# Six row buffers instead of eight for gathered expert rows in a hybrid decoder layer

## The chip, the cores and the metric

The kernel runs on one core of one Trainium2 chip. The metric is the device time of one execution in microseconds (us). Three runs of the kernel before took 3182.36, 3183.60 and 3184.69 us, so the median is 3183.6 us. The profile was taken in a separate execution on the same chip.

## The reference

The layer takes `x` of 1024 tokens by 1024 features in float32, puts 16 learned meta tokens ahead, and computes a mixer (differential attention beside a convolution group), an output projection, a residual add, and then an expert layer (PEER). It ends with a residual add and a final norm. All but a small part of the time of this kernel goes into the expert layer:

```python
def chunk(xt):                                # 128 tokens
    q = (xt @ wq).reshape(128, 8, 2, 128)     # 8 heads, two half queries
    s = jnp.einsum('thpk,hpnk->thpn', q, subkeys)
    s_top, i_top = lax.top_k(s, 16)           # top 16 of 128 keys, twice
    cand = s_top[:, :, 0, :, None] + s_top[:, :, 1, None, :]
    c_top, c_idx = lax.top_k(cand, 16)        # top 16 of the 256 sums
    e = i1 * 128 + i2                         # expert number, 0..16383
    gate = jax.nn.softmax(c_top, axis=-1)
    act = jax.nn.gelu(einsum('thkd,td->thk', u_tab[e], xt))
    return einsum('thk,thkd->td', gate * act, v_tab[e])
```

Each token picks 16 experts in each of 8 heads. For each pick, one row `u` of 1024 floats is needed for a dot product, and one row `v` of 1024 floats is added to the output with a weight. The two tables are stored side by side, so a pick fetches one row of 2048 floats (8 KB).

## The kernel before, in words

The mixer (`mixer_phase`) comes first and is not touched. The expert layer (`expert_phase`) works on 8 tiles of 128 tokens. Each tile has 8 heads, which makes 64 head steps, and each head step has 16 picks `k`. One pick of one head for all 128 tokens is one *gather*, numbered `g = 16 * m + k`, with `m` the head step. There are 1024 gathers, of 128 rows of 8 KB (1.0486 MB) each.

A gather goes through five engines in the order of `g`. Every engine's program is written out by hand, and semaphores count the gathers done.

- GpSimd (POOL, line 992) issues the indirect DMA into `ring[:, g % RING, :]`. Before that it waits at line 991 until the gather that held this buffer has been combined.
- VectorE (DVE, line 1229) waits until all 16 DMA engines have reported the gather, and computes the dot product of the `u` half with the tokens (`dot`).
- ScalarE (line 1083) takes the gelu of the dot products.
- VectorE (line 1239) builds a diagonal matrix of gate times gelu (`diagonal`). In its program `diagonal(g - LAG)` stands behind `dot(g)` with `LAG = 2`, so the diagonal of gather `g` is built only after the dot of gather `g + 2`.
- TensorE (PE, line 1345) adds the weighted `v` half to the accumulator in four matmuls (eight in the trace, since float32 runs as two passes), and reports the buffer free (`b_free`).

```python
if g >= RING:
    pool.wait_ge(b_free, g - RING + 1)                 # L991
pool.indirect_dma_start(out=ring[:, g % RING, :], ...) # L992
...
dve.wait_ge(b_row[g % RING], 16 * (g // RING + 1))     # L1228, dot
...
pe.wait_ge(b_diag, g + 1)                              # combine
...
ins.then_inc(b_free, 1)
```

Between these, the engines do the routing of the coming head steps. VectorE has one part of `route` after each dot (top 16 searches). TensorE has `queries` (line 1321, eight k tiles) in three portions behind the combines 0, 1 and 2 of every head step, `queries_t` behind combine 4, `key_scores` behind combine 6, and in heads 0 to 3 of the first seven tiles the output projection of the next tile (`project`, line 1302) behind the combines 5 and 12. TensorE works in program order, so a combine that stands behind one of these waits for it.

SyncE loads `mix_t` and `h_next` of the next tile and stores finished tiles; these go over the same 16 DMA engines as the gathers.

`RING` (line 39) is used at these places alone: the size of the tile `ring` (line 899), the number of semaphores `b_row` (954), the wait of POOL (990, 991), the buffer and semaphore of the gather (992, 994), the wait and buffer of the dot (1228, 1229), and the buffer that the combine reads (1346).

Of the kernel before, what the change touches and what calls it, by code (L numbers as in the profile page):

```python
# [35 lines left out]
TOPK = 16  # L36
QH = 128
CAND = TOPK * TOPK
RING = 8
DIAGS = 4  # L40

SEGS = [(0, 352), (352, 352), (704, 336)]
# [834 lines left out]
def expert_phase(nc, shared, x, mix_dram, g2, wq, table, g_final, out):  # L877

    ctx = ExitStack()
    with ctx:  # L880
        def sb(name, shape, dt=F32):
            return ctx.enter_context(nc.sbuf_tensor(name, shape, dt))
# [4 lines left out]
        def sem(name):  # L887
            return ctx.enter_context(nc.semaphore(name))
# [9 lines left out]
        gf_half = sb("gf_half", [P, 512])  # L898
        ring = sb("ring", [P, RING, 2 * D])
        xn = [sb("xn_even", [P, D]), sb("xn_odd", [P, D])]  # L900
# [52 lines left out]
        b_gate = sem("b_gate")  # L953
        b_row = [sem(f"b_row{r}") for r in range(RING)]
        b_free = sem("b_free")
# [19 lines left out]
        def _(pool):  # L975
# [10 lines left out]
            for g in range(NSTEPS * TOPK):  # L986
                m, k = divmod(g, TOPK)
                if k == 0:
                    pool.wait_ge(b_route, m + 1)
                if g >= RING:  # L990
                    pool.wait_ge(b_free, g - RING + 1)  # L991
                pool.indirect_dma_start(out=ring[:, g % RING, :], out_offset=None, in_=table[:, :],  # L992
                                        in_offset=bass.IndirectOffsetOnAxis(ap=e_row[m % 2][:, k:k + 1], axis=0)
                                        ).then_inc(b_row[g % RING], 16)

# [457 lines left out]
```

## Time and profile before

| | before |
|---|---|
| median of three runs | 3183.6 us |
| profiled execution, device time | 3180.26 us |
| its span, first to last instruction | 3178.5 us |
| PE busy | 2407.4 us (76%) |
| DVE busy | 2295.8 us (72%) |
| POOL busy | 1147.7 us (36%) |
| ACT busy | 710.0 us (22%) |
| mean granted TensorE clock | 0.833 |
| q0 (the gathers): packets, MB, share of 16 engines | 147456, 1073.81, 80.9% |

The profiled execution is 3.3 us (0.1%) below the median of the timed runs. Its last instruction ends 1.8 us before the device time does. Mixer and expert layer follow one another: the first gather is issued 577 us after the start, the last 3153 us after it.

In a row of the order of time, the first number is the start in us from the span's start and the second the duration; `x8` is the number of instructions merged, and the bracket gives how long the engine was idle before, and what ended it.

### The profile page before, as it was taken

The page shows a single profiled execution, that of the slowest core. Times are in us where ns is not written, and L with a number is a line of the kernel's source. Part 1 is how long each engine was busy: PE and PEld are TensorE (multiplying, and loading weights), DVE is VectorE, ACT ScalarE, POOL GpSimd, SP SyncE. Part 2 cuts the span into 40 slices and gives each one's busy share as a digit, 9 for nine tenths or more (in the row PEclk, how much of TensorE's full clock was granted, in tenths as well). Part 3 has the DMA queues.
Part 4 walks back from the last instruction along what each step waited for, and adds up shares of the span by engine and source line. Part 5 has one row for each costly group of instructions (what it writes and reads, how often), then busy time and mean ns, then how long its engine had stood idle before and what let it go on. Part 6 is the DMA issues. An engine that isn't in the chain of part 4 may idle for free.

```text
span 3178.5 us, 35285 instructions
## 1 busy us (share of the span) xinstructions
PE 2407.4 (76%) x11880; PEld 872.3 (27%) x11880; DVE 2295.8 (72%) x5927; ACT 710.0 (22%) x1963; POOL 1147.7 (36%) x1073
## 2 busy tenths in 40 slices
PE   8998977677777777777777777767777787767776
PEld 4655554221222222222222222222222222212111
DVE  1566673677777777777777777777777777777775
ACT  3143444112121212121212121212121111211111
POOL 1000000344434444444443344444444444444443
PEclk9999987888888888887888878787897788887776
DMA  3300001999999999999999999999999999999998
GB/s 109 119 27 27 20 7 34 397 426 426 426 413 416 426 424 409 419 425 420 419 418 426 422 416 412 422 425 424 417 420 422 421 415 420 420 425 417 422 422 337
DMA packets 184956, 1121.58 MB, mean 353 GB/s; under 512 B 19520, under 2 KB 45248, under 8 KB 53584
## 3 DMA queue, kind: packets, MB, share of 16 engines
q0 software_dynamic: 147456, 1073.81, 80.9%
q1 hardware_dynamic: 37328, 45.63, 4.2%
q8 instruction: 90, 1.47, 0.2%
q14 instruction: 82, 0.67, 0.1%
HBM read 1110.97 MB, written 8.39 MB: 352 GB/s over the span
## 4 chain that ended last, share of the span: by engine, by line
DMA 49%; PE 19%; issue 7%; DVE 5%; POOL 2%; ACT 0%; DVEq 0%; SPq 0%; POOLq 0%; ACTq 0%
DMA ring<-table,e_even 25%; DMA ring<-table,e_odd 24%; PE acc_even L1345 6%; PE acc_odd L1345 6%; PE qq_ps L1321 4%; PE proj L1302 3%; POOL ring L992 2%; DVE diag L1239 1%; DVE dots L1229 0%; DVE cand_t L1189 0%; DVE ring L1229 0%; DVE hot L1208 0%; DVE hot L1202 0%; DVE top_i L1172 0%; DVE top_i L1162 0%
## 5 line engine op out<-in xcount | busy, mean ns | idle before, releaser
L1345 PE MATMUL acc_odd<-ring,diag 64*64 64x512 f32 x4096 | 712.9, 778 | 342.5 <-DVE diag L1239 334.9
L1345 PE MATMUL acc_even<-ring,diag 64*64 64x512 f32 x4096 | 690.7, 755 | 341.4 <-DVE diag L1239 334.1
L1229 DVE CUSTOM_DVE_ANT_0 ring<-ring,xn_odd 128x1024 f32<-128x1024 f32 x512 | 627.5, 1226 | 305.2 <-DMA ring<-table,e_odd 155.1
L992 POOL DMA_INDIRECT ring<-table,e_even x512 | 557.1, 1088 | 774.7 <-PE acc_even L1345 363.3
L1229 DVE CUSTOM_DVE_ANT_0 ring<-ring,xn_even 128x1024 f32<-128x1024 f32 x512 | 627.5, 1226 | 285.1 <-DMA ring<-table,e_odd 147.5
L992 POOL DMA_INDIRECT ring<-table,e_odd x512 | 558.0, 1090 | 711.5 <-PE acc_even L1345 346.4
L1083 ACT ACTIVATE gelu<-dots 128x1 f32<-128x1 f32 x1024 | 207.6, 203 | 2081.8 <-DVE dots L1229 2066.0
L1345 PEld LDWEIGHTS acc_odd<-ring,diag 64*64 64x64 f32 x4096 | 126.0, 156 | 795.2 <-DVE diag L1239 740.6
L1345 PEld LDWEIGHTS acc_even<-ring,diag 64*64 64x64 f32 x4096 | 123.3, 153 | 766.4 <-DVE diag L1239 711.3
L1321 PE MATMUL qq_ps<-wq_rest,xnT_cur 128*128 128x256 f32 x896 | 266.1, 435 | 6.5 <-DMA wq_rest<-wq 6.5
L1321 PEld LDWEIGHTS qq_ps<-wq_rest,xnT_cur 128*128 128x128 f32 x896 | 175.7, 212 | 192.3 <-issue 164.6
L1239 DVE TENSOR_SCALAR diag<-pairs,gelu,gate_even 128x64 f32<-128x64 f32 x512 | 168.8, 330 | 0.0
L1239 DVE TENSOR_SCALAR diag<-pairs,gelu,gate_odd 128x64 f32<-128x64 f32 x512 | 167.9, 328 | 0.0
L558 DVE SCALAR_TENSOR_TENSOR y<-u_pad,cpar,y 128x1024 f32<-128x1024 f32 x120 | 158.7, 1323 | 6.8 <-DVE y L558 0.9
L733 PE MATMUL proj<-xnT,w_slot 128*128 128x352 f32 x512 | 158.1, 464 | 1.4 <-DVE yc L594 1.4
L1302 PE MATMUL proj<-w_out_s,mix_t 128*128 128x512 f32 x224 | 147.6, 794 | 0.0
L733 PEld LDWEIGHTS proj<-xnT,w_slot 128*128 128x128 f32 x512 | 97.2, 192 | 55.0 <-issue 5.1
L1083 ACT ACT_TABLE_LOAD x78 | 100.1, 1283 | 1.4
L619 DVE CUSTOM_DVE_ANT_0 z<-bankA,bias 128x264 f32<-128x264 f32 (+8 forms) x112 | 52.8, 506 | 62.2 <-PE bankA L744 61.8
L1229 DVE DVE_READ_ACCUMULATOR2_ANT dots<- 128x1 f32 x1024 | 84.4, 82 | 0.0
L1302 PEld LDWEIGHTS proj<-w_out_s,mix_t 128*128 128x128 f32 x224 | 51.4, 255 | 114.5 <-issue 114.5
L1057 ACT ACT_TABLE_LOAD x64 | 82.1, 1283 | 1.4
(190 smaller groups left out, 1936.0 us busy)
## 6 DMA issues: line engine op xcount, KB each, us to landing
w_slot<-w_in SPq DMA_DIRECT2D x16, 512.0 KB, 4.0
ring<-table,e_even POOLq DMA_INDIRECT x512
ring<-table,e_odd POOLq DMA_INDIRECT x512
wq_rest<-wq SPq DMA_DIRECT2D x1, 7168.0 KB, 21.9
w_out_s<-x SPq DMA_DIRECT2D x8, 512.0 KB, 4.0
w_out_s<-w_out SPq DMA_DIRECT2D x1, 4096.0 KB, 12.9
h_next<-x SPq DMA_DIRECT2D x8, 512.0 KB, 13.8
mix_t<-mix_dram SPq DMA_DIRECT2D x7, 512.0 KB
```

Source lines behind the costliest of these rows:

```text
L558: dve.scalar_tensor_tensor(out=y[:], in0=u_pad[:, META + k:META + k + SEQ], scalar=cp[:, k:k + 1], in1=y[:], op0=ALU.mult, op1=ALU.add).th ...
L619: dve.tensor_tensor_reduce(z[:, i % 2, c, lo:hi], banks[3 + c][:, 0:hi - lo], bias[:, off + lo:off + hi], 1.0, NEG, ALU.add, ALU.max, zmax ...
L733: ins = pe.matmul(banks[n][:, 0:w], w_slot[:, slot, k, :], xnT[:, k, lo:lo + w], start=(k == 0), stop=(k == KC - 1))
L992: pool.indirect_dma_start(out=ring[:, g % RING, :], out_offset=None, in_=table[:, :], in_offset=bass.IndirectOffsetOnAxis(ap=e_row[m % 2][ ...
L1057: act.activation(g_exp[:], c_top[:], ACT.Exp, bias=neg_top[:], accum_out=g_sum[:, 0:1]).then_inc(b_gexp, 1)
L1083: act.activation(gelu[:, k:k + 1], dots[:, k:k + 1], ACT.Gelu).then_inc(b_gelu, 1)
L1229: dve.tensor_tensor_reduce(ring[:, g % RING, 0:D], ring[:, g % RING, 0:D], xn[(m // PH) % 2][:], 1.0, 0.0, ALU.mult, ALU.add, dots[:, k:k ...
L1239: dve.tensor_scalar(diag[:, g % DIAGS, :], pairs[:, 0, :], gelu[:, k:k + 1], gate[m % 2][:, k:k + 1], ALU.mult, ALU.mult).then_inc(b_diag, 1)
L1302: ins = pe.matmul(proj[b][:], mix_t[:, k, :], w_out_s[:, k, HALF[b]], start=(k == 0), stop=(k == KC - 1))
L1321: ins = pe.matmul(q_ps, xnT[:, k, :], w, start=(k == 0), stop=(k == KC - 1))
L1345: ins = pe.matmul(acc[t % 2][ROWS[j], HALF[i]], diag[ROWS[i], g % DIAGS, :], ring[ROWS[i], g % RING, D + j * 512:D + (j + 1) * 512], start ...
```

## The change

Line 39 sets the number of row buffers. Everything that depends on it follows: the tile `ring` has six rows of 8 KB on each partition instead of eight, there are six semaphores `b_row`, and POOL issues gather `g` once combine `g - 6` is reported, not combine `g - 8`.

```diff
@@ -36,7 +36,7 @@
 TOPK = 16
 QH = 128
 CAND = TOPK * TOPK
-RING = 8
+RING = 6
 DIAGS = 4
 
 SEGS = [(0, 352), (352, 352), (704, 336)]
```

No instruction is added, removed or moved in the program of any engine.

## Rows read from the trace of the kernel before

**Rows 1.** The page, 40 slices of the span: busy tenths of the DMA engines.
```profile
DMA  3300001999999999999999999999999999999998
```

**Rows 2.** Stretch by window: length, engines' busy us (instructions), clock, DMA share, GB/s.
```profile
600.00:3150.00 2550.00, 1879.68 (x9796) 552.81 (x9794) 1957.05 (x5211) 484.73 (x1481) 1102.44 (x1013) 0.81 1.01 421
```

**Rows 3.** The waits, whole span: total us, times, longest us.
```profile
POOL ring L992 <- PE acc_even L1345: 709.7, 465, 7.1
...
DVE ring L1229 <- DMA ring<-table,e_odd: 302.6, 497, 2.4
...
POOL ring L992 <- issue: 54.6, 98, 5.2
```

**Rows 4.** Order of time, DVE: the first dot, two near the end, the last.
```profile
586.59 1.22 DVE L1229 CUSTOM_DVE_ANT_0 ring<-ring,xn_even 128x1024 f32<-128x1024 f32 x1
...
3132.29 1.23 DVE L1229 CUSTOM_DVE_ANT_0 ring<-ring,xn_odd 128x1024 f32<-128x1024 f32 x1 [0.98 <-DMA ring<-table,e_odd]
...
3161.72 1.23 DVE L1229 CUSTOM_DVE_ANT_0 ring<-ring,xn_odd 128x1024 f32<-128x1024 f32 x1 [0.97 <-DMA ring<-table,e_odd]
3165.13 1.22 DVE L1229 CUSTOM_DVE_ANT_0 ring<-ring,xn_odd 128x1024 f32<-128x1024 f32 x1 [1.96 <-DMA ring<-table,e_odd]
```

**Rows 5.** The chain that ended last: start us, us, what, from a gather's issue.
```profile
1492.67 10.19 DMA ring<-table,e_even
```

**Rows 6.** Order of time, 1502 to 1509 us: two dots, combines and issues.
```profile
1502.88 1.28 DVE L1229 CUSTOM_DVE_ANT_0 ring<-ring,xn_even 128x1024 f32<-128x1024 f32 x1 [0.45 <-DMA ring<-table,e_even]
...
1504.99 1.67 PE L1345 MATMUL acc_even<-ring,diag 64*64 64x512 f32 x8 [0.52 <-DVE diag L1239]
1505.31 1.23 DVE L1229 CUSTOM_DVE_ANT_0 ring<-ring,xn_even 128x1024 f32<-128x1024 f32 x1 [0.37 <-DMA ring<-table,e_even]
...
1506.98 0.94 POOL L992 DMA_INDIRECT ring<-table,e_odd  x1 [1.23 <-PE acc_even L1345]
...
1507.26 1.09 PE L1345 MATMUL acc_even<-ring,diag 64*64 64x512 f32 x8 [0.59 <-DVE diag L1239]
...
1508.65 1.17 POOL L992 DMA_INDIRECT ring<-table,e_odd  x1 [0.73 <-PE acc_even L1345]
```

**Rows 7.** Order of time, POOL: the first gather and gather 8.
```profile
576.97 1.13 POOL L992 DMA_INDIRECT ring<-table,e_even  x1 [24.32 <-DVE e_even L1215]
...
593.85 0.94 POOL L992 DMA_INDIRECT ring<-table,e_even  x1 [7.05 <-PE acc_even L1345]
```

**Rows 8.** Windows from the first gather's issue, columns as in rows 2.
```profile
577.00:578.50 1.50, 1.50 (x6) 1.24 (x6) 0.00 (x0) 0.00 (x0) 1.20 (x2) 0.73 0.00 0
578.50:582.00 3.50, 2.55 (x13) 1.69 (x12) 0.00 (x0) 1.41 (x3) 2.71 (x3) 1.00 0.91 300
```

**Rows 9.** Order of time: dot of pick 4, issue after combine 2; heads 1, 2, 7.
```profile
1605.80 1.23 DVE L1229 CUSTOM_DVE_ANT_0 ring<-ring,xn_odd 128x1024 f32<-128x1024 f32 x1 [0.65 <-DMA ring<-table,e_odd]
...
1612.11 1.20 POOL L992 DMA_INDIRECT ring<-table,e_odd  x1 [1.56 <-PE acc_odd L1345]
...
1645.47 1.23 DVE L1229 CUSTOM_DVE_ANT_0 ring<-ring,xn_odd 128x1024 f32<-128x1024 f32 x1 [0.66 <-DMA ring<-table,e_even]
...
1650.52 0.94 POOL L992 DMA_INDIRECT ring<-table,e_even  x1 [0.58 <-PE acc_odd L1345]
...
1846.57 1.23 DVE L1229 CUSTOM_DVE_ANT_0 ring<-ring,xn_odd 128x1024 f32<-128x1024 f32 x1 [0.65 <-DMA ring<-table,e_odd]
...
1851.90 1.67 POOL L992 DMA_INDIRECT ring<-table,e_odd  x1 [0.83 <-PE acc_odd L1345]
```

**Rows 10.** Order of time, head 0: combines 6 and 13 behind the projection, same tile.
```profile
1573.83 1.22 DVE L1229 CUSTOM_DVE_ANT_0 ring<-ring,xn_odd 128x1024 f32<-128x1024 f32 x1
...
1575.89 2.97 PE L1302 MATMUL proj<-w_out_s,mix_t 128*128 128x512 f32 x4
...
1580.18 0.94 POOL L992 DMA_INDIRECT ring<-table,e_even  x1 [2.05 <-PE acc_odd L1345]
...
1591.49 1.23 DVE L1229 CUSTOM_DVE_ANT_0 ring<-ring,xn_odd 128x1024 f32<-128x1024 f32 x1 [0.90 <-DMA ring<-table,e_even]
...
1597.05 0.94 POOL L992 DMA_INDIRECT ring<-table,e_odd  x1 [3.17 <-PE acc_odd L1345]
```

## What the change is predicted to do

> **What bounds the kernel now.** I read the page first. In its 40 slices the DMA engines stand at nine tenths from the eighth slice to the last [rows 1]; that is the whole expert layer. The window over it gives a mean DMA share of 1.01 at 421 GB/s, while PE is busy for 1880 of 2550 us and DVE for 1957 [rows 2]. So the layer goes at the pace at which gathers land. The waits say the same from both ends of the ring: POOL waits for combines (709.7 us in 465 waits, and a second such row of 697.7 us in 460 for the other accumulator), that is, for a free buffer; the dots wait for landings (302.6 us in 497 waits, with a second row of 279.5 us in 456) [rows 3]. Both can be true at once because a queue of issued gathers lies between. The question is how much of it two buffers are.
>
> The pace comes from the dots. From 3132.29 to 3161.72 lie 12 intervals of 2.45 us [rows 4]. Over the whole layer it is (3165.13 - 586.59) / 1023 = 2.52 us [rows 4], since other transfers and hiccups take their part.
>
> The length of the queue comes from the chain of waits. One gather is issued at 1492.67 and lands 10.19 us later [rows 5], which is more than four intervals of 2.45 us. The dot begins at once, at 1502.88. The second half of the loop begins there: the dot of gather g+2 is started, diagonal g follows it on DVE, combine g follows on PE at 1504.99, and POOL issues into the freed buffer at 1506.98 [rows 6]. I call this the return: 1506.98 - 1502.88 = 4.10 us. One gather later it is 1508.65 - 1505.31 = 3.34 us [rows 6]. The difference is the combine: eight matmuls take 1.67 us in the first case and 1.09 in the second [rows 6]; PE is granted the upper level in part of the time only, 0.81 as a mean of the layer [rows 2].
>
> **The change, part by part.** The number of instructions and bytes stays the same. All that moves is when POOL may issue.
>
> *The lap.* A buffer's loop runs from the landing of gather g+2 over the return to the issue of gather g+RING, and from there to its landing. With eight buffers one lap covers 8 - 2 = 6 gathers, with six it covers 4. DMA stays fed if the lap fits into the time in which DMA moves as many gathers: 6 x 2.45 = 14.7 us before, 4 x 2.45 = 9.8 us after. Check on before: 10.19 + 4.10 = 14.3 us, so the queue takes up all the slack there is, as it should.
>
> *The least time from issue to landing.* The trace of before never shows a gather that lands as fast as it can while it matters, since a queue always stands ahead of it. It must be bounded. From below: the first gather is issued at 576.97 [rows 7] and no byte is moved until 578.5 [rows 8]; 1.5 us for that and 2.45 us for its own bytes, and a little for the report, make about 4.3 us. From above: between 578.5 and 582.0 the engines moved 3.5 x 300 = 1.05 MB [rows 8], one gather's worth, so the first gather needs at least 582.0 - 577.0 = 5.0 us on an empty queue, and the slowest of 16 engines comes after the mean. A descriptor job that takes POOL 1.17 us [rows 6], and others that take longer, come on top; I set 6.0 us as the other end. I take 5.2 us, next to the row of the first gather. Both ends are kept for the range.
>
> *What is left for the return.* 9.8 - 5.2 = 4.6 us. The two returns of rows 6 (4.10 and 3.34 us) fit into it with 0.5 to 1.3 us to spare, so most gathers cost nothing. With eight buffers the same sum left 14.7 - 5.2 = 9.5 us. What no longer fits are the late returns, those where combine g stands behind other work on PE. When several returns in a row are late, the gathers behind share one stall, because each starts from its own landing and these were already on time; so I count the longest of a lot. One tile (from 1559 to 1880 us) stands for all.
>
> *Lots behind the queries.* The return of combine 2 is 1612.11 - 1605.80 = 6.31 us in head 1, 1650.52 - 1645.47 = 5.05 in head 2, and 1851.90 - 1846.57 = 5.33 in head 7 [rows 9]. In the other five heads it is at or under the budget. Over 4.6 us these are 1.71, 0.45 and 0.73, together 2.9 us a tile, and 8 tiles make 23 us.
>
> *Lots behind the projection* (heads 0 to 3 of seven tiles). Combine 6 in head 0 stands behind four matmuls of 2.97 us [rows 10] and returns after 1580.18 - 1573.83 = 6.35 us, 1.75 over. Combine 13 in head 0 returns after 1597.05 - 1591.49 = 5.56 us [rows 10], 0.96 over, and there are three such in the tile. Together 1.75 + 3 x 0.96 = 4.6 us a tile, and 7 tiles make 32 us.
>
> *The scattered rest.* POOL was idle for 54.6 us in 98 waits before which nothing released it, 5.2 us the longest [rows 3]. Some of these fall on a return. I allow 12 us for them, a fifth, since only the long ones pass the spare time.
>
> *The start and the end.* With six buffers gather 6 waits for combine 0. That is the point at which gather 8 is issued now, 593.85 [rows 7]; its first bytes come 1.5 us later, at 595.4. One gather's worth of bytes is through at 582.0 [rows 8], so six last until 582.0 + 5 x 2.45 = 594.3 on the mean engine, and longer on the slowest. I put the start at 0, between -1 and +3. Behind the last gather the path is the same.
>
> The sum is 23 + 32 + 12 = 67 us on the profiled execution of 3180.3 us, 3247 us. The timed median is 3.3 us higher, so 3251 us.
>
> *A rule of the skill.* The first gather's bytes come 1.5 us after its issue [rows 7, 8]. The Trainium skill, page "DMA: Bandwidth & Descriptors", section "Anatomy of one DMA — SWDGE (gpsimd) path", puts a transfer issued by GpSimd at some 2.0 us fixed plus bytes over 436 GB/s, most of the fixed part being the report at the end. By that page's figures a gather would need about 4.4 us, an estimate, which is 0.6 us less than the 5.0 us at which the rows of the first gather arrive; by that rule the sum would come near that of the first rival, and the trace speaks against it only for an empty queue.
>
> **The rivals.**
>
> *Rival 1: the lead of a gather is hidden by the one ahead.* While one gather's packets still run, the setup of the next may overlap fully, and the least time is the lower bound, 4.3 us. For it: the slow first bytes (300 GB/s in rows 8 against 421 in rows 2) belong to an empty queue. Against it: a late return is just what empties the queue. The budget is then 5.5 us. The queries lots cost 6.31 - 5.5 = 0.8 us a tile (6 us in all), the projection lots 0.85 + 3 x 0.06 = 1.0 us a tile (7 us in all), the rest some 5. That gives +18 us, 3202 us. If the rest of the slack is more generous still, it ends within 6 us of before, which is no change.
>
> *Rival 2: the lap doesn't fit for ordinary gathers either.* At 6.0 us the budget is 3.8 us, and a return at PE's lower level (4.10 us) is 0.3 over. Then 0.3 / 4 = 0.075 us is lost on every gather of such stretches, some 45 us if they are 600 of 1024. The queries lots grow to 2.51 + 1.25 + 1.53 and three smaller ones, some 7 us a tile (56 in all), the projection lots to 2.55 + 3 x 1.76 = 7.8 us a tile (55 in all), the rest 25. Together +180 us, 3365 us. For it: the 16 DMA engines don't end together, a landing needs the last of them, and an engine that is ahead can't stay ahead when the queue is short, so that each hiccup of any engine would show. Against it: ordinary returns at the upper level (3.34 us) would still fit.
>
> *Rival 3, the other side: a shorter queue lets the transfers run closer to their best pace.* The mean interval is 2.52 us against 2.45 undisturbed, 0.07 x 1023 = 72 us in all. The other transfers' bytes explain some of it: 421 GB/s x 2550 us = 1073.6 MB, less 1013 gathers of 1.0486 MB (1062.2 MB), leaves 11.3 MB, or 27 us [rows 2]. If the remaining 45 us came from five gathers queued at once, and three did better, the time could fall by up to 45 us, and it decides if the lots above cost less than that: 3140 to 3180 us, 3160 as its middle. Against it: the DMA share is 1.01, so the engines don't idle, and nothing shows that depth makes them slower.
>
> That the change does nothing would need POOL to issue late for another reason. Its waits are for combines [rows 3], so the wait it is given decides.
>
> **How the numbers follow.** What a measurement of this kernel can tell from no change is about 0.2%, 6 us. The forecast, late returns no longer hidden, +35 to +120 us: 0.52. Rival 1, +0 to +35: 0.25, of which 0.10 lies within 6 us. Rival 2, +120 us and more: 0.18. Rival 3: 0.05. Slower is 0.52 + 0.15 + 0.18 = 0.85, same 0.10, faster 0.05. The range goes from 3190 us, where "no change" ends, to 3345 us, above which I see a quarter of rival 2 (0.05); outside lie 0.05 + 0.10 + 0.05 = 0.20.
>
> **What would show it.** In the changed kernel the time from issue to dot should be 5 to 6 us, not 10; the return should stay at 3.3 to 4.5 us for ordinary gathers. The DMA share of the layer should fall from 1.01 to about 0.98, with dips after combines 0 to 2 of the slow heads and after combines 6 and 13 of heads 0 to 3. The waits of the dots for the gathers should grow by about the loss, from 582 us to some 650. Intervals outside the late lots should stay at 2.45 us. If they are longer everywhere, rival 2 is right and the least time from issue to landing was taken too short; if the dips are there but the landings don't move, rival 1 is. A loss that falls on the route or the gelu, or a mean clock far from 0.81, would show a mechanism that I haven't seen.

## The result, and the profile after

| | before | after |
|---|---|---|
| median of four runs | 3183.4 us | 3686.4 us (3676.6 to 3694.2) |
| ratio | | 1.158, 95% interval 1.1564 to 1.1595 |
| profiled execution, its span | 3178.5 us | 3674.8 us |
| mean granted TensorE clock | 0.833 | 0.765 |

The change costs 503 us. The prediction was 3251 us with a range up to 3345 us: right in direction, but the loss was seven and a half times the 67 us of its sum, and far outside the range. The number of instructions is the same, 35285.

The first view is again the 40 slices of the page. They answer to [rows 1], with the bytes below.
```profile
DMA  3210009999999999999999999999999999999998
GB/s 128 76 35 17 12 22 345 352 361 349 348 343 348 360 359 362 361 353 356 353 352 341 350 346 355 348 358 355 338 345 354 360 336 351 339 347 382 359 354 300
```
The DMA engines still show nine tenths in every slice of the expert layer. Read alone, this row says that nothing has changed. The bytes say otherwise: about 350 GB/s where the window of [rows 2] had 421. The window over the layer of the changed kernel gives both in one row (columns as in [rows 2]).
```profile
600.00:3640.00 3040.00, 2067.05 (x9790) 588.44 (x9788) 1952.56 (x5208) 483.71 (x1480) 1096.52 (x1011) 0.74 0.95 353
```
Share times length over gathers is the time for which a mean DMA engine is busy for one gather. Before, it was 1.01 x 2550 / 1013 = 2.54 us [rows 2]; now it is 0.95 x 3040 / 1011 = 2.86 us. The interval between gathers went from 2.52 us [rows 4] to 3.00 us ((3659.74 - 586.34) / 1023, below). So of the 0.48 us lost on each gather, some 0.3 us are time in which DMA engines count as busy without moving more, and only the rest is idle DMA. Shares are given to 0.01, which is 0.03 us here.
```profile
586.34 1.22 DVE L1229 CUSTOM_DVE_ANT_0 ring<-ring,xn_even 128x1024 f32<-128x1024 f32 x1
...
3659.74 1.22 DVE L1229 CUSTOM_DVE_ANT_0 ring<-ring,xn_odd 128x1024 f32<-128x1024 f32 x1 [1.08 <-DMA ring<-table,e_odd]
```
The waits answer to [rows 3].
```profile
POOL ring L992 <- PE acc_even L1345: 978.7, 484, 11.8
POOL ring L992 <- PE acc_odd L1345: 959.1, 485, 6.0
...
DVE ring L1229 <- DMA ring<-table,e_odd: 553.0, 511, 3.6
DVE ring L1229 <- DMA ring<-table,e_even: 538.9, 484, 4.3
```
The dots wait for gathers for 1092 us where they waited for 582. The 510 us more are the loss. DVE's own work is as before.

The time from issue to landing fell, as it must with fewer gathers ahead in the queue. The page now gives a median of it, 7.9 us; the chain of waits has single ones, here 7.51 us where [rows 5] had 10.19.
```profile
ring<-table,e_even POOLq DMA_INDIRECT x512, 7.9
```
```profile
1503.74 7.51 DMA ring<-table,e_odd
```
The return (from the dot of gather g+2 to the issue into the buffer that combine g frees) is what it was. In the order of time, the dot at 1511.28 leads to the combine at 1513.40 and the issue at 1514.79, 3.51 us; the median over all gathers is 4.2 us, and 4.1 us before (means 4.25 and 4.17). So the lap is 7.9 + 4.2 = 12.1 us, and over four gathers that is the 3.0 us measured.
```profile
1511.28 1.23 DVE L1229 CUSTOM_DVE_ANT_0 ring<-ring,xn_even 128x1024 f32<-128x1024 f32 x1 [1.05 <-DMA ring<-table,e_odd]
...
1513.40 1.09 PE L1345 MATMUL acc_even<-ring,diag 64*64 64x512 f32 x8 [0.91 <-DVE diag L1239]
1514.79 0.94 POOL L992 DMA_INDIRECT ring<-table,e_odd  x1 [0.86 <-PE acc_even L1345]
```

**The lead.** The order of time shows which gathers land late. I call lead the time by which a gather is issued ahead of the landing of the one before it. These rows are POOL's issues and DVE's dots; a dot that waited for DMA starts as its gather lands.
```profile
1450.92 0.94 POOL L992 DMA_INDIRECT ring<-table,e_even  x1 [3.58 <-PE acc_even L1345]
...
1452.35 1.25 POOL L992 DMA_INDIRECT ring<-table,e_even  x1 [0.49 <-PE acc_even L1345]
...
1454.01 1.22 DVE L1229 CUSTOM_DVE_ANT_0 ring<-ring,xn_even 128x1024 f32<-128x1024 f32 x1 [0.39 <-DMA ring<-table,e_even]
...
1459.14 1.23 DVE L1229 CUSTOM_DVE_ANT_0 ring<-ring,xn_even 128x1024 f32<-128x1024 f32 x1 [3.08 <-DMA ring<-table,e_even]
...
1461.59 1.23 DVE L1229 CUSTOM_DVE_ANT_0 ring<-ring,xn_even 128x1024 f32<-128x1024 f32 x1 [0.66 <-DMA ring<-table,e_even]
```
The gather issued at 1450.92 is 3.09 us ahead of the landing at 1454.01, and lands 5.13 us after it, at 1459.14. The next one, issued at 1452.35, is 6.79 us ahead of that landing, and follows it after 2.45 us. The windows over the first of the two show how DMA spends that time.
```profile
1452.50:1454.00 1.50, 0.33 (x4) 0.21 (x8) 1.12 (x6) 0.20 (x1) 1.10 (x1) 1.00 0.95 240
1454.00:1455.50 1.50, 0.76 (x8) 0.00 (x0) 1.49 (x4) 0.20 (x1) 0.44 (x1) 1.00 1.05 415
1455.50:1457.00 1.50, 0.89 (x8) 0.22 (x8) 0.56 (x2) 0.00 (x0) 0.54 (x1) 0.75 0.97 202
```
The share is near 1 in all three, while the rate is 240, 415 and 202 GB/s: busy engines, in two of the three with about half the bytes. (The view books a packet's time and bytes whole in the window in which it starts.)

I did the same for every pair of neighbouring gathers, in four kernels. The table has the median time between two landings, in us, with the number of pairs, worked out from the rows of issues and dots. Leads under 1 us and over 9 us are left out; five buffers have 31 pairs with 0 to 1 us, and 4.9 us between the landings.

| lead, us | 8 buffers | 7 | 6 | 5 |
|---|---|---|---|---|
| 1 to 2 | | | 4.24 (11) | 4.15 (137) |
| 2 to 3 | | 3.86 (3) | 3.66 (49) | 3.37 (467) |
| 3 to 4 | | 3.21 (23) | 3.28 (212) | 3.10 (306) |
| 4 to 5 | 2.44 (1) | 2.96 (73) | 3.03 (282) | 3.07 (54) |
| 5 to 6 | 2.49 (15) | 2.45 (327) | 2.50 (300) | 2.45 (19) |
| 6 to 7 | 2.45 (54) | 2.45 (414) | 2.45 (136) | 2.46 (3) |
| 7 to 8 | 2.45 (238) | 2.44 (140) | 2.45 (24) | |
| 8 to 9 | 2.45 (440) | 2.44 (35) | | |

The four columns are nearly one curve: in a row they differ by 0.3 us where there are many pairs. From a lead of some 5.5 us on, gathers land at the full pace of 2.45 us; with six buffers the median is 2.5 us for leads of 5.0 to 5.5 us, and the mean 2.7. The kernels described below with another lag or gate lie close to it too: at a lead of 4 to 5 us they have 2.99 (five buffers, lag 1), 3.08 (eight with POOL's gate at six) and 3.10 us (the short combine), and 2.5 us at 5 to 6. With eight buffers the median lead was 8.6 us and one pair in 1023 had less than 5 us; with six the median is 4.9 us, and 556 pairs have less than 5. That one pair landed at the full pace in spite of a lead of 4.2 us, so a single late gather in a long queue is not what the curve describes.

### The profile page after: what moved, and what is told of

The parts are those of the page before. It is cut to its first block, busy times and chain, and to the rows that moved or that the text cites. A ratio compares the mean times of both kernels' runs of the same rounds, so it can differ in the third digit from the quotient of the medians.

```text
span 3674.8 us, 35285 instructions
## 1 busy us (share of the span) xinstructions
PE 2598.6 (71%) x11880; PEld 909.6 (25%) x11880; DVE 2292.5 (62%) x5927; ACT 709.1 (19%) x1963; POOL 1141.8 (31%) x1073
## 4 chain that ended last, share of the span: by engine, by line
DMA 48%; PE 21%; issue 9%; DVE 6%; POOL 1%; ACT 0%; SPq 0%; DVEq 0%; POOLq 0%; ACTq 0%
DMA ring<-table,e_odd 24%; DMA ring<-table,e_even 24%; PE acc_odd L1345 7%; PE acc_even L1345 7%; PE qq_ps L1321 3%; DVE diag L1239 2%; PE proj L1302 2%; POOL ring L992 1%; DVE top_i L1172 1%; DMA wq_rest<-wq 1%; PE s_ps L1336 1%; DVE cand_t L1189 1%; DVE ring L1229 1%; DVE dots L1229 1%; DVE hot L1202 0%
## 5 line engine op out<-in xcount | busy, mean ns | idle before, releaser
L1345 PE MATMUL acc_odd<-ring,diag 64*64 64x512 f32 x4096 | 783.4, 850 | 494.0 <-DVE diag L1239 492.8
L1345 PE MATMUL acc_even<-ring,diag 64*64 64x512 f32 x4096 | 765.5, 831 | 495.3 <-DVE diag L1239 494.5
L992 POOL DMA_INDIRECT ring<-table,e_odd x512 | 548.1, 1070 | 987.1 <-PE acc_even L1345 488.5
L1345 PEld LDWEIGHTS acc_odd<-ring,diag 64*64 64x64 f32 x4096 | 133.9, 168 | 1001.8 <-DVE diag L1239 956.6
L1345 PEld LDWEIGHTS acc_even<-ring,diag 64*64 64x64 f32 x4096 | 130.7, 164 | 978.7 <-DVE diag L1239 930.0
L1321 PE MATMUL qq_ps<-wq_rest,xnT_cur 128*128 128x256 f32 x896 | 285.0, 460 | 7.4 <-DMA wq_rest<-wq 7.4
L1321 PEld LDWEIGHTS qq_ps<-wq_rest,xnT_cur 128*128 128x128 f32 x896 | 186.4, 224 | 205.4 <-issue 173.4
L1302 PE MATMUL proj<-w_out_s,mix_t 128*128 128x512 f32 x224 | 162.9, 867 | 0.0
```

Source lines behind the costliest of these rows:

```text
L1302: ins = pe.matmul(proj[b][:], mix_t[:, k, :], w_out_s[:, k, HALF[b]], start=(k == 0), stop=(k == KC - 1))
L1321: ins = pe.matmul(q_ps, xnT[:, k, :], w, start=(k == 0), stop=(k == KC - 1))
L1345: ins = pe.matmul(acc[t % 2][ROWS[j], HALF[i]], diag[ROWS[i], g % DIAGS, :], ring[ROWS[i], g % RING, D + j * 512:D + (j + 1) * 512], start ...
```

## The experiments

Two explanations stood against each other after the result. The *late returns* are the prediction's: only gathers whose combine stands behind other work drain the queue. The *short lead* says that ordinary gathers are issued too late at this depth already, and that DMA itself then goes slower. The expectations below call the second "Theory B" from the second set on; in the first one, "Theory A" is the lap law as such (the interval is the time of a lap, issue to landing plus return, over the RING - LAG gathers in it, if that is more than DMA needs) and "Theory B" a step that comes with any queue shorter than eight.

**Depth: seven, five and three buffers.**
```diff
-RING = 8
+RING = 7        # or 5, or 3
```


> Seven row buffers, all else as before. A lap (return plus issue to landing) covers 7 - 2 = 5 gathers. Theory A (the lap law): the interval between gathers is the larger of 2.52 us (DMA-bound) and (issue to landing + return) / 5 = (7.9 + 4.2) / 5 = 2.42 us, so it is near the edge: 3190 to 3300 us. Theory B (the loss of six buffers is a step that comes with any queue shorter than eight): over 3400 us.

> Five row buffers: a lap covers 3 gathers. Lap law with the issue to landing of the changed kernel (7.9 us): (7.9 + 4.2) / 3 = 4.03 us, 587 + 1024 x 4.03 = 4710 us. If those 7.9 us are mostly queueing behind other gathers, and shrink to the least time seen (5.4 us): 3.2 us, 3860 us. In between, 7 us: 3.73 us, 4410 us.

> Three row buffers: a lap covers one gather, so each gather is issued after the one before has landed and goes over DMA engines that are empty. Its issue to landing is that of a lone gather. If the 7.9 us of the changed kernel are what every gather that finds drained engines pays: interval 12.1 us, some 13000 us. If a lone gather lands in 5.4 us: interval 9.6 us, 10400 us, and the 7.9 us come from gathers that share the engines.

Measured: 3248 us with seven (ratio 1.021, interval 1.019 to 1.024), 4156 us with five (1.306), 10669 us with three (3.35). There is no step at eight; the loss grows with each buffer taken away, from 65 us with seven to 503 with six and 973 with five. Five buffers lie between the three values named, with a lap of 6.2 + 4.2 us on the mean. Three buffers come near the 10400 us named for a gather that lands as if alone. The windows over the layer, with seven, five and three buffers:
```profile
600.00:3200.00 2600.00, 1881.17 (x9778) 548.22 (x9777) 1951.47 (x5198) 484.74 (x1477) 1090.51 (x1009) 0.81 1.00 411
```
```profile
600.00:4100.00 3500.00, 2225.42 (x9771) 616.30 (x9774) 1956.64 (x5203) 484.33 (x1479) 1158.40 (x1008) 0.67 0.87 305
```
```profile
600.00:10600.00 10000.00, 2786.73 (x9828) 757.96 (x9828) 1936.65 (x5227) 487.25 (x1489) 950.37 (x1015) 0.53 0.32 108
```
The same product as above gives 2.58, 3.02 and 3.15 us of busy DMA engine per gather, against 2.54 with eight and 2.86 with six. The same bytes cost more the fewer gathers are on their way.

The records of single packets in these traces say which part is longer. A gather moves its rows in 128 packets of 8 KB, and in every one of these runs the median packet takes 0.309 us. Some take two or three times as long:

| | 8 buffers | 7 | 6 | 5 | 3 |
|---|---|---|---|---|---|
| packets over 0.5 us | 0.7% | 1.5% | 7.1% | 11.1% | 13.8% |
| time over 0.309 us a packet, us per gather and engine | 0.03 | 0.07 | 0.34 | 0.49 | 0.61 |
| first to last of a gather's 16 engine reports, median us | 3.5 | 1.9 | 1.9 | 0.6 | 0.6 |

From eight buffers to six the second row rises by 0.31 us, which is all of the rise in busy time (2.54 to 2.86 us). With three buffers it is plain which packets are the long ones: the sixteen of a gather that start first take 0.80 us in the median, and from the thirty-third on the median is 0.309 again.

Three buffers also measure the term that the prediction had to bound, a gather alone on empty engines:
```profile
4999.91 0.94 POOL L992 DMA_INDIRECT ring<-table,e_even  x1 [9.22 <-PE acc_odd L1345]
...
5005.56 1.23 DVE L1229 CUSTOM_DVE_ANT_0 ring<-ring,xn_odd 128x1024 f32<-128x1024 f32 x1 [7.99 <-DMA ring<-table,e_even]
```
That is 5.65 us to the dot; the page has 5.5 us as the median to the landing. The windows of 0.5 us over it (three buffers again) show how it starts.
```profile
5000.00:5001.50 1.50, 0.00 (x0) 0.00 (x0) 0.00 (x0) 0.00 (x0) 0.85 (x1) 0.50 0.00 0
5001.50:5002.00 0.50, 0.00 (x0) 0.00 (x0) 0.00 (x0) 0.00 (x0) 0.00 (x0) 0.50 1.46 246
5002.00:5002.50 0.50, 0.00 (x0) 0.00 (x0) 0.00 (x0) 0.00 (x0) 0.00 (x0) 0.50 0.47 131
5002.50:5003.00 0.50, 0.00 (x0) 0.00 (x0) 0.00 (x0) 0.00 (x0) 0.00 (x0) 0.50 0.84 311
5003.00:5003.50 0.50, 0.00 (x0) 0.00 (x0) 0.00 (x0) 0.00 (x0) 0.00 (x0) 0.50 1.02 426
...
5004.50:5005.00 0.50, 0.00 (x0) 0.00 (x0) 0.00 (x0) 0.00 (x0) 0.00 (x0) 0.50 0.40 164
```
Nothing moves for 1.5 us, then come 1.5 us at 131 to 311 GB/s, then the full rate, and the last packets start before 5005. (A share over 1 is a packet booked whole in the window in which it starts.) A gather alone thus begins slowly, and it holds the engines for some 3.3 us, not 2.45. With eight buffers there is little of this start: 0.7% of long packets.

**Is it the buffers, or the lap?** Two kernels have the lap of the changed kernel with another number of buffers. One has five buffers, and the diagonal one dot earlier:
```diff
-RING = 8
+RING = 5
-LAG = 2
+LAG = 1
```


> Five row buffers, and diagonal g stands behind dot g + 1 instead of g + 2: a lap covers 5 - 1 = 4 gathers, as in the changed kernel with its six buffers. Lap law: 3620 to 3740 us, the time of the changed kernel. If the number of buffers itself decides (how many gathers can be on their way), it is as slow as five buffers with the old lag, over 4000 us.

The other has all eight buffers, and only POOL waits as with six:
```diff
-                if g >= RING:
-                    pool.wait_ge(b_free, g - RING + 1)
+                if g >= 6:
+                    pool.wait_ge(b_free, g - 6 + 1)
```


> Eight buffers, but POOL waits for combine g - 6 as it does with six. If the wait is what costs the time: the changed kernel's 3650 to 3730 us. If the buffers themselves cost it (their number or their place in memory): 3180 to 3200 us.

Measured: 3704 us and 3681 us, beside the 3686 us of the change, both in the range of the lap law. Neither the number of buffers nor their place in memory matters by itself beyond some 20 us. What matters is how many gathers a lap covers: RING - LAG, or what POOL's wait makes of it. A third way to a lap of four, eight buffers with LAG = 4, gave no time: that program deadlocks.

**Do the late returns carry the loss?** TensorE does one k tile in eight of the queries and of the projection:
```diff
 def queries(r, k):
...
+                if r >= 2 and k != KC - 1:
+                    return
...
 def project(p, k):
...
+                if k != KC - 1:
+                    return
```


> Six buffers, and TensorE does one of the eight k tiles of the queries and of the projection (from head step 2 and tile 1 on), so that no combine stands behind long other work. Seven eighths of these products are left out of the computation. Theory A (the late returns alone drain the queue, ordinary returns fit, as predicted): back to 3185 to 3230 us. Theory B (a gather that finds drained DMA engines takes longer, and this holds for ordinary gathers at this depth): 3400 to 3600 us.

Measured: 3664 us (3661 and 3667, where the changed kernel's four runs were 3677 to 3694), 22 us less than with them. The late returns did go: nine in ten returns of combine 1 were under 6.25 us, and are now under 4.21 us. So the mechanism that the whole forecast was made of is worth some 20 us of 503, and the late-returns theory falls. The result lies outside the range given for Theory B too, 3400 to 3600 us, which credited the late returns with too much.

**Is the ordinary return worth anything?** The first try was half a combine:
```diff
-                for i, j in QUARTERS:
+                for i, j in QUARTERS[:4 if (h == PH - 1 and k == TOPK - 1) else 2]:
```


> Six buffers, and a combine does two of its four matmuls (half of the weighted sum is left out, but for the last pick of a tile). The ordinary return is some 0.5 to 0.9 us shorter, the late ones still come. Lap law with a constant issue to landing: 0.12 to 0.22 us less on each interval of 3.00 us, 3460 to 3560 us. Theory B allows more, since a queue that drains less also restarts less: down to 3300 us. Theory A (late returns alone): 3600 us or more, since they stay.

> Six buffers with both cuts: no long work ahead of a combine, and half a combine. Every return is then some 3.0 to 3.5 us, and with the 5.5 us of a lone gather (three buffers) a lap takes 8.5 to 9.0 us where four intervals of DMA-bound work take 9.8. If the draining is all there is to it, it is DMA-bound again: 3180 to 3210 us. If something else bounds a short queue, 3300 us or more.

Measured: 3692 and 3649 us. These two say nothing on the question, since the edit did not do what it was meant to: the return kept its median of 4.2 us. In the trace of the second, four matmuls take the time that eight took (eight take 1.98 us in the changed kernel; the granted clock is 0.5, the lower level, in both stretches):
```profile
1500.11 1.97 PE L1349 MATMUL acc_even<-ring,diag 64*64 64x512 f32 x4 [1.48 <-DVE diag L1239]
```
The matmuls of a combine are on four different quarters of the array, and by these times they run side by side. A shorter matmul does what fewer did not:
```diff
-                    ins = pe.matmul(acc[t % 2][ROWS[j], HALF[i]], diag[ROWS[i], g % DIAGS, :],
-                                    ring[ROWS[i], g % RING, D + j * 512:D + (j + 1) * 512],
+                    n = 512 if (h == PH - 1 and k == TOPK - 1) else 128
+                    ins = pe.matmul(acc[t % 2][ROWS[j], i * 512:i * 512 + n], diag[ROWS[i], g % DIAGS, :],
+                                    ring[ROWS[i], g % RING, D + j * 512:D + j * 512 + n],
```


> Six buffers; each of the four matmuls of a combine covers 128 of its 512 columns (three quarters of the weighted sum are left out, but for the last pick of a tile), since leaving out two matmuls of four did not shorten a combine. The ordinary return falls by 0.8 to 1.4 us. Lap law with a constant 7.9 us from issue to landing: 0.2 to 0.35 us less per interval, 3330 to 3480 us. Theory B (DMA itself goes slower because each gather comes too shortly ahead of its turn): the time gained goes into the lead, and the time falls part of the way towards seven buffers, 3400 to 3580 us. If the return does not matter: 3650 us or more.

```profile
1502.64 0.70 PE L1346 MATMUL acc_even<-ring,diag 64*64 64x128 f32 x8 [2.16 <-DVE diag L1239]
```
Measured: 3530 us. The median return fell from 4.20 to 3.12 us and the interval by 0.14 us, from 3.00 to 2.86. Had the 7.9 us been constant, 1.08 / 4 = 0.27 us would have gone. Instead the gathers stand in the queue longer (8.3 us), and their lead rises from 4.9 to 5.4 us in the median. That is inside the range of the short lead, and outside that of the lap law with constants. The window of this kernel again shows the busy time per gather falling, to 0.98 x 2890 / 1009 = 2.81 us:
```profile
600.00:3490.00 2890.00, 1300.77 (x9762) 660.71 (x9762) 1969.08 (x5202) 482.73 (x1478) 1302.38 (x1009) 0.61 0.98 370
```

**Gathers in pairs.**
```diff
-                if g >= RING:
-                    pool.wait_ge(b_free, g - RING + 1)
+                if g >= RING and g % 2 == 0:
+                    pool.wait_ge(b_free, g - RING + 2)
```


> Six buffers; POOL waits only at even gathers, for both buffers, and issues two gathers back to back. The first of a pair is issued one return later than it could be, so a lap covers 3.5 gathers on the mean. Lap law alone: 12.1 / 3.5 = 3.46 us, some 4100 us. If what costs is a slow start of each gather that comes shortly ahead of its turn, the second of a pair has none, and half of the slow starts go: 3500 to 3800 us.

Measured: 4126 us. The lap law's 4100 us is hit, in part by luck: its 12.1 us over 3.5 gathers are not what happened. The lap of a pair's first gather covers three, and took 4.3 us of return and 6.0 us to the dot in the median: 10.3 / 3 = 3.4 us, which is the interval. The hope of Theory B's side was wrong in its reasoning: the first of a pair has a lead of only 2.5 us in the median and lands 3.6 us after the one before, and the second, issued 1.24 us later, has a short lead as well (4.4 us, and 3.2 us between the landings). For example
```profile
1644.86 0.94 POOL L992 DMA_INDIRECT ring<-table,e_odd  x1 [7.02 <-PE acc_even L1345]
...
1646.10 1.28 POOL L992 DMA_INDIRECT ring<-table,e_odd  x1 [0.30 <-issue]
...
1650.57 1.22 DVE L1229 CUSTOM_DVE_ANT_0 ring<-ring,xn_even 128x1024 f32<-128x1024 f32 x1 [3.61 <-DMA ring<-table,e_odd]
...
1653.78 1.23 DVE L1229 CUSTOM_DVE_ANT_0 ring<-ring,xn_even 128x1024 f32<-128x1024 f32 x1 [1.15 <-DMA ring<-table,e_odd]
```
The second has a lead of 4.47 us and lands 3.21 us after the first, a little above the curve's 3.0 us.

**Giving the lead back with the lag.**
```diff
-LAG = 2
+LAG = 1        # with RING = 6, and with RING = 8
```


> Six buffers, as in the changed kernel, and diagonal g behind dot g + 1: a lap covers 5 gathers, as with seven buffers and the old lag. Expected is the time of that kernel, 3235 to 3270 us, 430 us under the changed kernel. If the later dot was what kept DVE or the diagonal in time and its loss costs: 3300 us or more.

> Eight buffers, and diagonal g behind dot g + 1: a lap covers 7 gathers, one more than before. A gather is then issued some 6 x 2.45 - 4.2 = 10.5 us ahead of the landing of the one before it, where the runs so far show the full pace from about 6 us on. So nothing is left to gain: 3176 to 3188 us. If the 0.07 us by which the mean interval lies above the undisturbed one come from a queue that is still too short: 3130 to 3170 us.

Measured: 3266 us with six buffers (ratio 1.024, interval 1.020 to 1.028), which is 420 us under the changed kernel and near the seven buffers of the old lag; and 3177.6 us with eight (ratio 0.9989, interval 0.9980 to 0.9998, eleven runs). The last is 0.1% under the kernel before, less than the 0.2% that was set as no change. A seventh gather in the lap finds next to nothing left to hide. Ten buffers at the old lag can't be had: one tile then needs 4096 bytes on each partition of the on-chip memory, and 736 are left.

## Why the prediction was wrong

*What bounds the kernel, and the lap.* Right. The lap covers RING - LAG gathers, the wait that POOL is given decides, and DMA was the bound. The kernels with five buffers and with the gate show this. The check of the lap, 10.19 + 4.10 = 14.3 us, rested on one gather that landed soon; the median from issue to dot was 11.1 us, so the lap was 15.2 us, about six intervals of 2.52 us. That changes nothing in what follows.

*The least time from issue to landing.* 5.2 us was taken, with bounds of 4.3 and 6.0 us. Measured alone it is 5.5 us in the median, within the bounds. This is not where the error lies.

*What is left for the return.* This is the step that failed. The prediction put it: "9.8 - 5.2 = 4.6 us. The two returns of rows 6 (4.10 and 3.34 us) fit into it with 0.5 to 1.3 us to spare, so most gathers cost nothing." This takes it that a gather which comes in time not to leave DMA without work lands at the full pace. In terms of the lead: 5.2 - 2.45 = 2.75 us would have been enough. The curve says some 5.5 us. At a lead of 3 to 5 us, which the prediction counted as free, landings are 3.0 to 3.3 us apart. So the budget fails for ordinary gathers; they are late by the measure that counts. The loss on each was put at nothing, and is 0.48 us on the mean.

The curve also gives the time, about; it is made from four of these kernels, so this is a check of the account and no forecast. With n gathers in a lap, the lead is (n - 1) times the interval less the return. At n = 4, an interval of 2.45 us would leave 3 x 2.45 - 4.2 = 3.15 us, for which the curve has 3.3 us; an interval of 3.0 us leaves 4.8 us, for which it has 3.0 us. That is where it settles. At n = 5 it is 4 x 2.5 - 4.2 = 5.8 us, almost free; at n = 6 it is 8.05 us, free; at n = 3 it settles near 3.45 us with 2.7 us of lead. The four measured mean intervals are 3.00, 2.58, 2.52 and 3.47 us.

*The lots behind queries and projection,* 23 + 32 us in the sum: the late returns are there, and taking them away gave back 22 us. Why not 55 is not shown; I suppose that in a loop that is already short a late return moves only a part of its lateness on. The +12 us for the rest can't be told apart.

*The start,* put at 0, between -1 and +3 us. The dots of gathers 6 and 7 started at 599.74 and 603.17, where the kernel before had them at 599.78 and 602.23. Fine for the first, and the loss begins with the second.

*The rivals.* The result falls in the class of rival 2, +120 us and more, which had a chance of 0.18. Rival 2 had the right place, the lap of ordinary gathers, and even named a short queue in which the 16 engines no longer make up for each other. But it was priced at +180 us, with a fixed 6.0 us against 9.8, 0.075 us a gather; the measured 0.48 us is six times that. DMA's own time per gather was held fixed in every case. Rival 1 (the lead is hidden) and rival 3 (a shorter queue is faster) have the wrong sign of just this effect: the busy time per gather rises from 2.54 to 2.86 us. That it could change was considered downwards only.

*A rule of the skill.* The estimate of 4.4 us from the Trainium skill, page "DMA: Bandwidth & Descriptors", section "Anatomy of one DMA — SWDGE (gpsimd) path", is too low here for a lone gather of 1.05 MB by 1.1 us: 5.5 us measured. The page has bytes over 436 GB/s for all of them, and the trace shows the first 1.5 us of movement at 131 to 311 GB/s.

*What would show it.* The test on the intervals was set well: "If they are longer everywhere, rival 2 is right". Its second half, "and the least time from issue to landing was taken too short", is true by 0.3 us only (5.5 us against 5.2), and 0.3 us does not explain a lap that is 2.3 us too long. The undisturbed 2.45 us do occur in the changed kernel, but behind a long lead. The time from issue to dot was to be 5 to 6 us and is 7.9; with a return as forecast, that is the failed step once more. The DMA share came out at 0.95, not 0.98. The granted clock of the layer fell from 0.81 to 0.74, which was named as a sign of another mechanism; but the mean return grew by 0.08 us only, 0.02 us on each interval, and the kernel with the short combine is faster at 0.61.

One view of the kernel before could have warned. POOL issued one gather late there, at 1934.96, 6.1 us after the one before, and the window behind it is
```profile
1936.00:1938.00 2.00, 2.00 (x16) 0.83 (x18) 1.59 (x5) 0.44 (x2) 1.18 (x2) 1.00 0.74 188
```
The engines are busy at 0.74 and move 188 GB/s: 0.74 of 426 would be 315. A queue that runs short costs rate as well as idle time. The late gather's dot still came 2.44 us after the one before, and the next one 2.63 us after it, so next to nothing was lost. The 16 engines' reports of the gather two places ahead show why: ten came by 1934.03 and the last at 1936.65. A landing needs the last of them, and the engines that were behind still had work queued.

What stays open is what inside DMA makes a gather with a short lead slow. The windows show busy engines at half their rate at the start of a gather and where one gather ends and the next begins, and the packets show that some take 0.5 us and more in place of 0.309. Engines that run out of work between two gathers are the smaller part: the first packet of a lone gather starts 1.6 us after its issue, and for 886 of 1021 gathers of the changed kernel no engine had reported the gather before by then; their mean interval is 2.90 us all the same, against 3.00 for all. Whether a long packet waits for descriptors or for its first reads from memory, no run here tells apart.

## What to carry to other kernels

Count a ring by its lap: buffers less the gathers that the consumer lags behind (RING - LAG). Then compare how early each transfer is issued with how early it must be, and take the second from runs with several depths, not from the least latency; here 5.5 us of lead kept the full pace where the latency alone asked for 3. Cutting the consumer's lag by one is worth a whole buffer: here it gave back 420 us with the same six buffers. And read the DMA share together with the bytes: nine tenths in every slice stood for 421 GB/s and for 353.

## What the runs showed of the hardware

- A DMA engine can count as busy and move half of what it otherwise does. Busy time per gather of the same bytes was 2.54, 2.58, 2.86, 3.02 and 3.15 us with laps of 6, 5, 4, 3 and 1 gathers.
- The added busy time is in single packets: of the 8 KB packets of the gathers, whose median is 0.309 us in each of these runs, 0.7% took over 0.5 us with eight buffers, 7.1% with six and 13.8% with three.
- The 16 engines drift apart in a long queue: from the first to the last report of a gather there are 3.5 us in the median with eight buffers, 1.9 with six and 0.6 with three.
- A gather of 128 rows of 8 KB, alone, takes 5.5 us to land: 1.5 us before any byte, 1.5 us at 131 to 311 GB/s, then 426 GB/s.
- Of four matmuls on different quarters of the array, leaving out two saves nothing (1.97 us for four passes, 1.98 us for eight); a quarter of the columns brings them to 0.70 us, all at a granted clock of 0.5.
